# Strassen's scheme for the feed-forward up products: seven block products for two output tiles in place of eight

## What is computed

```python
def sq_relu_mlp(h, w_up, w_down):                 # first model, D_FF = 4096
    return jnp.square(jax.nn.relu(h @ w_up)) @ w_down
...
D_FF_2 = 2816                                     # second model
FFN_CONV = 3
```

## Time and profile before

| | |
|---|---|
| median of 3 runs | 2861.84 us (2861.54 to 2865.23) |
| the profiled execution, span | 2860.9 us |
| TensorE busy | 2799.9 us, 98% |
| weight loads (PEld) busy | 2463.7 us, 86% |
| POOL, DVE, ACT busy | 1376.9, 1479.0, 1000.0 us |
| granted TensorE clock | 0.993 of full speed over the span |

### The profile page before, as it was taken

One profiled execution on the slowest core, in us unless ns is written; L12 is line 12 of the kernel. 1 busy time (PEld: TensorE's weight loads), 2 busy tenths in 40 slices (PEclk: granted clock), 3 DMA queues, 4 the chain that ended last, 5 costly groups with the idle time before them and its releaser, 6 DMA issues.

```text
span 2860.9 us, 43560 instructions
## 1 busy us (share of the span) xinstructions
PE 2799.9 (98%) x17428; PEld 2463.7 (86%) x17428; DVE 1479.0 (52%) x2439; ACT 1000.0 (35%) x1489; POOL 1376.9 (48%) x1748
## 2 busy tenths in 40 slices
PE   9989999999999999999899999999999999999999
PEld 7768888877788888998799999999989799999887
DVE  8955322267532227897644544233798745444241
ACT  4453222255422224443353322223443345322221
POOL 6426554555654556542225555456542225555554
PEclk9999999999999999999999999999999999999999
DMA  5103322222232224223324222222322243332322
GB/s 187 60 25 103 102 96 89 97 97 79 96 96 92 96 99 126 98 74 98 85 83 142 88 89 92 94 85 93 113 81 78 65 118 116 98 102 89 102 90 74
DMA packets 122630, 270.79 MB, mean 95 GB/s; under 512 B 22864, under 2 KB 57040, under 8 KB 122192
## 3 DMA queue, kind: packets, MB, share of 16 engines
q1 hardware_dynamic: 73104, 245.98, 26.0%
q10 hardware_dynamic: 49344, 22.19, 2.8%
HBM read 249.52 MB, written 18.61 MB: 94 GB/s over the span
## 4 chain that ended last, share of the span: by engine, by line
PE 42%; issue 29%; POOL 24%; DVE 4%; POOLq 0%; ACT 0%; DMA 0%; ACTq 0%; DVEq 0%
PE acc L666 33%; POOL w_lo L638 24%; PE acc L1078 2%; PE acc L1059 2%; PE aux L1059 2%; PE aux L1092 1%; DVE index_score L2706 1%; DVE best L2699 1%; PE acc L1286 0%; PE aux L969 0%; PE acc L1092 0%; PE acc L920 0%; PE aux L1278 0%; PE aux L951 0%; PE acc L1148 0%
## 5 line engine op out<-in xcount | busy, mean ns | idle before, releaser
L638 POOL TENSOR_TENSOR w_lo<-w_raw,w_hi 128x256 fp32r<-128x256 f32 x1744 | 1376.7, 821 | 1467.8 <-ACT w_hi L1320 1467.0
L666 PE MATMUL acc<-n_hi,w_hi 128*128 128x264 f32 (+1 forms) x2824 | 756.9, 323 | 2.3 <-DVE index_k L2398 1.3
L666 PE MATMUL acc<-n_lo,w_hi 128*128 128x264 f32 (+1 forms) x2824 | 748.0, 320 | 0.0
L666 PE MATMUL acc<-n_hi,w_lo 128*128 128x264 f32 (+1 forms) x2824 | 746.0, 319 | 0.0
L1320 ACT ACTIVATE w_hi<-w_raw 128x1024 fp32r<-128x1024 f32 (+1 forms) x436 | 454.1, 1043 | 615.2 <-PE acc L666 561.5
L666 PEld LDWEIGHTS acc<-n_hi,w_hi 128*128 128x128 f32 x2824 | 470.4, 188 | 59.8 <-issue 15.0
L666 PEld LDWEIGHTS acc<-n_lo,w_hi 128*128 128x128 f32 x2824 | 467.3, 188 | 40.9 <-issue 2.6
L666 PEld LDWEIGHTS acc<-n_hi,w_lo 128*128 128x128 f32 x2824 | 467.2, 188 | 38.3
L2214 DVE TENSOR_TENSOR x<-x,acc 128x512 f32<-128x512 f32 (+1 forms) x144 | 99.7, 692 | 562.6 <-PE acc L666 519.3
L666 PE MATMUL acc<-hidden_lo,w_hi 128*128 128x512 f32 (+1 forms) x1040 | 343.3, 358 | 0.0
L666 PE MATMUL acc<-hidden_hi,w_lo 128*128 128x512 f32 (+1 forms) x1040 | 342.7, 357 | 0.0
(11 more groups left out here) (484 smaller groups left out, 3750.0 us busy)
## 6 DMA issues: line engine op xcount, KB each, us to landing
w_raw<-in_stream SPq DMA_DIRECT2D x420, 512.0 KB, 3.5
unit_blocks<-unit_scratch ACTq DMA_DIRECT2D x26, 256.0 KB, 4.0
w_raw<-in_stream SPq DMA_DIRECT2D x16, 384.0 KB, 3.0
unit_scratch<-unit_staged ACTq DMA_DIRECT2D x20, 256.0 KB, 2.8
saved_x<-x SPq DMA_DIRECT2D x2, 2112.0 KB, 10.5
x<-saved_x SPq DMA_DIRECT2D x16, 264.0 KB, 2.7
saved_gates<-root ACTq DMA_DIRECT2D x12, 264.0 KB, 2.1
unit_scratch<-unit_staged ACTq DMA_DIRECT2D x1, 2560.0 KB, 13.4
```

Source lines behind the costliest of these rows:

```text
L638: i = pool.tensor_tensor(wl[:, slot, s], raw[:, slot, s], wh[:, slot, s].bitcast(F32), ALU.subtract)
L666: last = pe.matmul(o, w[:, p % W_SLOTS, P * b:P * b + P], r, start=(b == 0 and i == 0), stop=(b == n - 1 and i == 2))
```

## The change

Two output tiles of an up product (in the second model a gate tile and its partner) are made together as a 2x2 block product: the weights of two pieces are four half pieces of four blocks each, a11 and a12 (first piece), a21 and a22 (second), and the rows are cut in two halves of 256 (264). In place of eight half products, seven are made (the form of Strassen's scheme with shared sums): with a11, a12 and a22, and with four sums of half pieces, s1 = a21 + a22, s2 = s1 - a11, s4 = a12 - s2, s3 = a21 - a11. DVE makes the weight sums (`weight_sum_of`) from the raw fp32 pieces, 128x512 each; ACT and POOL then split all seven as they split whole pieces before. The sums of the normed activations that the scheme needs are made once at each stage's start: 20 DVE instructions of 128x256 (264) (`token_sums`), four ACT copies and four DVE subtractions of 128x1024 (1056) (`token_sum_low`).

Three of the products serve two results. ACT copies them out of PSUM when they are done (`keep_product`), TensorE goes on adding to the same bank, and DVE makes results as bank plus kept copy (`pair_product`).

The ring now is in half pieces, eight of them (`Order`), and every "op" is a half piece of 12 matmuls' weight blocks. One pair is a11 s1 a12 s2 s4 s3, then the two halves of a down piece, then a22, and in the first model two more down halves. The hidden chunks have four tiles now, and a down piece holds half the rows for two output tiles, so that each down op is 12 matmuls of 512 columns (24 of 264 in `layer0`). The first four tiles of `mlp0` and `mlp1` and the first three of the second model's (six pieces) are made whole, as before. That leaves 14 pairs in each of `mlp0`, `mlp1` and 19 in each of `layer0`, `layer1`. In `layer1` both up halves are made for all 528 rows. POOL's loop is written out. The other stages keep their work; their waits are counted in ops.

A cut of the diff, with the loops of the second model's feed-forward (the first model's are alike, with relu and square):

```diff
--- before.py
+++ after.py
@@ -111,18 +111,29 @@
...
-def mlp_order():
...
-FFN_THIRDS = [(0, 8), (8, 16), (16, FT2)]
-FFN_ORDER = [("up", 0), ("up", 1), ("down", 0), ("up", 2), ("down", 1), ("down", 2)]
+MLP_CHUNKS = [(n, n + 4) for n in range(0, FF // P, 4)]
+FFN_CHUNKS = [(0, 3), (3, 6)] + [(n, n + 4) for n in range(6, FT2, 4)]
...
+def feed_steps(stage):
+
+    chunks, gated = chunks_of(stage), stage.startswith("layer")
+    order = [("whole", 0, n) for n in range((2 if gated else 1) * chunks[0][1])]
+    for e in range(1, len(chunks)):
+        n = (chunks[e][1] - chunks[e][0]) // (1 if gated else 2)
+        for i in range(n):
+            order.append(("pair", e, i))
+            order += [("down", e - 1, k) for k in range(4 * i // n, 4 * (i + 1) // n)]
+    return order + [("down", len(chunks) - 1, k) for k in range(4)]
...
+FACTORS = ("a11", "s1", "a12", "s2", "s4", "s3", "a22")
+SUMS = ("s1", "s2", "s4", "s3")
+LATER = 2
...
+        def add(kind, piece, part, halves=1):
+            nonlocal place
+            place += place % halves
+            self.turned.append(max(in_ring[(place + n) % (2 * W_SLOTS)] for n in range(halves)))
+            self.ops.append((kind, piece, part))
+            self.place.append(place % (2 * W_SLOTS))
+            for n in range(halves):
+                in_ring[(place + n) % (2 * W_SLOTS)] = len(self.ops)
...
+        for stage, end in zip(STAGES, ends):
+            feed = stage.startswith(("mlp", "layer"))
+            steps = feed_steps(stage) if feed else []
...
+                    add("whole", p, 0, 2)
+                    p += 1
+                elif what == "pair":
+                    self.op_of[p] = len(self.ops)
+                    for f in FACTORS[:6]:
+                        add(f, p, pair)
+                    kept = (p, pair)
+                    pairs.append(p)
+                    pair += 1
+                    p += 2
+                else:
+                    self.op_of[p] = len(self.ops)
+                    for part in range(2):
+                        add("down", p, part)
+                    p += 1
+                    if kept:
+                        add(FACTORS[6], *kept)
+                        kept = None
...
+        found = [n + 1 for n, (kind, piece, _) in enumerate(self.ops) if piece == p or (piece == p - 1 and kind == "a22")]
+        paired = [n + 1 for n, (kind, piece, _) in enumerate(self.ops) if piece == p and kind == "s3"]
+        return paired[0] if paired else max(found)
...
+    def weights_of(o):
+
+        kind, p, part = order.ops[o]
...
+        if kind in ("a11", "a12"):
+            return raw[:, p % RAW_SLOTS, half * (kind == "a12"):half * (kind == "a12") + half]
+        if kind == "s3":
+            return raw[:, (p + 1) % RAW_SLOTS, 0:half]
+        if kind == "a22":
+            return raw[:, (p + 1) % RAW_SLOTS, half:2 * half]
+        return weight_sum[:, SUMS.index(kind), :]
...
         for p in range(RAW_SLOTS, pieces):
-            sp.wait_ge(w_lo, p - RAW_SLOTS + 1)
+            sp.wait_ge(w_lo, order.freed(p - RAW_SLOTS))
...
+        for o, (kind, p, part) in enumerate(order.ops):
+            slot, at = order.half(o)
+            n = width_of(o)
+            source = weights_of(o)
+            pool.wait_ge(w_hi, o + 1)
+            for a in range(0, n, 2 * P):
+                z = min(a + 2 * P, n)
+                i = pool.tensor_tensor(wl[:, slot, at + a:at + z], source[:, a:z],
+                                       wh[:, slot, at + a:at + z].bitcast(F32), ALU.subtract)
+            i.then_inc(w_lo, 1)
...
+        def pairs_and_downs(stage, cols):
...
+            def banded(o, bank, hi, lo, opens):
+
+                slot, at_ = order.half(o)
+                for b in range(KT // 2):
+                    for i, (w, v) in enumerate(((wh, hi), (wh, lo), (wl, hi))):
+                        mm = pe.matmul(aux[:, bank, 0:width], w[:, slot, at_ + P * b:at_ + P * b + P], v[:, b, :],
+                                       start=(opens and b == 0 and i == 0), stop=(b == KT // 2 - 1 and i == 2),
+                                       skip_group_check=True)
+                mm.then_inc(w_used, 1)
...
+            for o in feed["ops"]:
+                kind, p, u = order.ops[o]
...
+                if kind == "a11":
+                    if u >= 2:
+                        pe.wait_ge(pair_out, out + 4 * (u - 1))
+                    banded(o, X_BANK[u % 2], nh[:, low, parts[0]], nl[:, low, parts[0]], True)
...
+                    banded(o, Y_BANK, nh[:, high, parts[0]], nl[:, high, parts[0]], True)
+                elif kind == "s2":
+                    if u == 0:
+                        pe.wait_ge(t_ready, sums + 2)
+                    pe.wait_ge(product_kept, kept + 3 * u + 1)
+                    banded(o, X_BANK[u % 2], th[:, 1, :, 0:width], tl[:, 1, :, 0:width], False)
+                elif kind == "s4":
+                    pe.wait_ge(product_kept, kept + 3 * u + 2)
+                    banded(o, Z_BANK, nh[:, high, parts[1]], nl[:, high, parts[1]], False)
+                elif kind == "s3":
...
+                elif kind == "a22":
+                    if u == 0:
+                        pe.wait_ge(t_ready, sums + 4)
+                    pe.wait_ge(pair_out, out + 4 * u + 3)
+                    banded(o, X_BANK[u % 2], th[:, 3, :, 0:width], tl[:, 3, :, 0:width], False)
...
+        def split_one():
+
+            o = at["split"]
+            kind, p, u = order.ops[o]
...
+                act.wait_ge(w_sum, c.next(w_sum))
...
+                act.wait_ge(landed[p % RAW_SLOTS], 16 * (p // RAW_SLOTS + 1))
+            if order.turned[o]:
+                act.wait_ge(w_used, order.turned[o])
+            n = width_of(o)
+            act.activation(wh[:, slot, at_:at_ + n], weights_of(o), ACT.Copy).then_inc(w_hi, 1)
+            at["split"] = o + 1
+
...
+        def split_before(o):
...
+            while at["split"] < len(order.ops):
                 q = at["split"]
...
-                at["split"] = q + 1
+                if order.turned[q] + (LATER if order.ops[q][0] in SUMS else 0) > o:
+                    return
+                split_one()
...
+        def token_sums_high(stage):
...
+            parts = halves_of(stage)
+            width = parts[0].stop - parts[0].start
+            for n in range(4):
+                act.wait_ge(t_sum, c.next(t_sum))
+                act.activation(th[:, n, :, 0:width], tf[:, n, :, 0:width], ACT.Copy).then_inc(n_hi, c.made(n_hi))
+
+        def keep_product(o, u, width):
+
+            kind = order.ops[o][0]
+            n = ("a11", "s1", "s2").index(kind)
+            act.wait_ge(w_used, o + 1)
+            if u:
+                act.wait_ge(pair_out, c.at(pair_out) + 4 * (u - 1) + (1, 3, 2)[n])
+            bank = Z_BANK if kind == "s1" else X_BANK[u % 2]
+            act.activation(kept_product[:, n, 0:width], aux[:, bank, 0:width], ACT.Copy)\
+                .then_inc(product_kept, c.made(product_kept))
...
+            for o in feed["ops"][:-KT]:
+                kind, p, u = order.ops[o]
+                split_before(o)
+                if kind in ("a11", "s1", "s2"):
+                    keep_product(o, u, HALF)
+                if kind == "s1" and u:
+                    hidden_high(whole + u - 1)
+                if kind == "s3":
+                    gate_silu(whole + u)
+            hidden_high(whole + feed["pairs"] - 1)
...
+            difference = [step(dve.tensor_tensor(t1[k], x[:, k, second], x[:, k, first], ALU.subtract)) for k in low]
...
+                made.append(ended(k, dve.tensor_scalar(t1[k], t1[k], gains(k), None, ALU.mult)))
...
+                made2.append(ended(k, dve.scalar_tensor_tensor(t2[k], x[:, high[k], second], gains(high[k]), t1[k],
+                                                               ALU.mult, ALU.subtract)))
...
+        def token_sum_low(stage, n):
+
+            width = halves_of(stage)[0].stop - halves_of(stage)[0].start
+            dve.wait_ge(n_hi, c.next(n_hi))
+            dve.tensor_tensor(tl[:, n, :, 0:width], tf[:, n, :, 0:width], th[:, n, :, 0:width].bitcast(F32), ALU.subtract)\
+                .then_inc(t_ready, c.made(t_ready))
...
+        def weight_sum_of(stage, u, name):
...
+                    dve.wait_ge(landed[q % RAW_SLOTS], 16 * (q // RAW_SLOTS + 1))
+            if name != "s3" and at["split"][n]:
+                dve.wait_ge(w_lo, at["split"][n])
+            at["split"][n] = order.index[name, p, u] + 1
...
+            s1, s2, s4 = (weight_sum[:, k, :] for k in range(3))
+            if name == "s1":
+                i = dve.tensor_tensor(s1, a21, a22, ALU.add)
+            elif name == "s2":
+                i = dve.tensor_tensor(s2, s1, a11, ALU.subtract)
+            elif name == "s4":
+                i = dve.tensor_tensor(s4, a12, s2, ALU.subtract)
+            else:
+                i = dve.tensor_tensor(a21, a21, a11, ALU.subtract)
+            i.then_inc(w_sum, c.made(w_sum))
```

(67 more changed lines are left out.)

705 lines of the change are left out of this document (469 added, 236 removed).

## The result

The changed kernel takes 2896.06 us (median of 4 runs, 2894.46 to 2899.78) against 2861.7 before (4 runs, 2861.54 to 2865.23): a ratio of 1.0125, 95% interval 1.0111 to 1.0140, or 34 us slower. Run again on another chip it took 2896.31 against 2860.88, 1.0127 [1.0112, 1.0143]. The forecast was 2906.

What follows compares the result with a forecast made beforehand. The prediction took TensorE to set the pace before the change, its share 100% in the feed-forwards. Forecast: 2861.8 - 24.4 + 15.6 + 26.6 + 20 + 6 + 0.9 = 2906.5, so 2906 us; range 2812 to 2948.

Steps and rivals of the forecast that it cites:

- first-model pairs: mlp0 and mlp1: each pair goes from 22.27 us to 21.4, TensorE needing 21.10; 28 pairs, -24.4 us.
- second-model pairs: layer0 and layer1: each pair takes 18.4 us, from 17.58 and 17.00; +15.6 and +26.6 us.
- four starts: Start of each feed-forward stage: DVE's queue of token sums and weight sums delays s3; 5 us each, +20.
- ends of stages: Last down products: DVE needs 0.85 us more than it gets, seven times in mlp1, +6; elsewhere 0 to +2.
- whole pieces: layer1's three pieces made whole, now at 264 columns: 72 slightly dearer matmuls, +0.9 us.
- narrow-matmul rival: 256-column matmuls can't go below 0.1221 us, so first-model pairs take 0.29 us more: 2915 us, chance 0.04.
- the port's 18.1: Second-model pair: POOL's 12.6 us and DVE's 5.5 on SBUF add up if they always take turns.
- The chain: Second-model pair: dependent DVE steps, then ACT's splits before the kept product's copy, then TensorE's s2 and s4: 18.8 us.
- The signs: Expected profile: first-model pairs 21.1 to 21.6 us, second-model 18 or more, POOL over 90% busy there, DVE's sums 1.2.
- TensorE bound: POOL and DVE mostly miss each other; second-model pairs take 16.1 and 15.9 us: 2788 us, chance 0.16.
- Full chain: All DVE's port instructions collide and waits add up; second-model pairs take 19.3 us: 2940 us, chance 0.20.
- Half way: Second-model pairs take some 17.2 us, with 15 us for the starts: 2856 us, chance 0.20.

Runs made afterwards that it cites:

- experiment 1: Changed kernel with ACT copying out the kept product before splitting the next half pieces, in the second model's pairs: 2887.2 us.
- experiment 2: Changed kernel with POOL making only half the low parts of the weights in the second model's pairs (result wrong, measures a cost): 2836.73 us.
- experiment 3: Changed kernel with the edits of experiment 1 and experiment 2 together (result wrong, measures a cost): 2829.75 us.
- experiment 8: Version 6 with DVE waiting at the start of mlp0 and mlp1 for POOL's low part of s1 before its next long instruction: 2859.82 us, 1.0000.
- experiments 4: Changed kernel with ACT allowed to split a weight sum one op earlier, all through: 2892.0 us.
- version 6: Changed kernel with the scheme in mlp0 and mlp1 only, layer0 and layer1 as before, and ACT's sum splits one op earlier: 2850.45 us, 0.9967.
- 7: Version 6 with DVE's weight sums moved earlier at the stage's start and ACT keeping products first in the first model too: 2852.78 us, 0.9972.
- experiment 9: Changed kernel with four fills with zeros in place of each stage's 20 token sums (result wrong, measures a cost): 2879.26 us.

## Why the prediction was right, and where its terms were off

The direction was right, and so was the mechanism of the largest term, the port that bounds the second model's pairs. That the total came within 10 us is luck: the pairs were 11 and 20 us better than forecast, and the starts 23 us worse.

| term | predicted | measured |
|---|---|---|
| first-model pairs, 28 | -24.4 | -35.6 |
| second-model pairs, 38 | +42.2 | +22 |
| four starts | +20 | +43 |
| ends of stages | +6 | +7.7 |
| whole pieces | +0.9 | not separable |
| unchanged stages | 0 | -3.7 |

*First-model pairs.* Measured 21.0 us, which is TensorE's 84 + 48 matmuls: 28 x (21.0 - 22.27) = -35.6. TensorE's 21.10 was right to 0.1 us, and 256 columns took 0.118 us. The 0.3 us for imperfect interleaving was not needed, with POOL at 92%. The narrow-matmul rival fell. The 98 ns for 256 columns, my estimate between the figures of the Trainium skill (TensorE: Matmul & The Clock Gate, "Back-to-back issue gap"), is contradicted by the measured 118 ns, and its 131 ns at 512 columns by the 232.

*Second-model pairs.* The port bounds them, as predicted, but at 17.3 us and not 18.4. This is the term that was mis-sized, in two steps. First, the shared time: with POOL full (experiment 1) a pair takes 17.1 us and not the port's 18.1, which is 12.6 of POOL's own and so 4.5 of DVE's 5.5; not all of DVE's instructions collided (L2701 kept 679 ns). The chain adds 0.2 us to that, where I had put 0.3 on the 18.1. (Its own list sums to 18.7 and not 18.8, and the 1.19 us read from the earlier trace rows is 0.1 less than the 0.70 and 0.59 of which it was said to be made; neither moves the forecast.) Second, I took all 19 pairs of a layer to have cost 17.58 or 17.00 us before; seven of them have down pieces of three blocks, which cost TensorE 16.12 and 15.61 (12 down matmuls of 264 columns fewer, or 6 of 512). The pair hardly shrinks with them (17.4 to 17.6), though the port isn't full there: POOL is busy 88% of the time (92.87 us from 1661 to 1766 us), and experiment 1 takes 108.7 us for six of the seven to 104.9, experiment 2 to 94.8. What holds these seven is port and chain together, in shares that no run separates. So twelve pairs changed by -0.28 and +0.35 us each, -3 and +4 us, and nearly all of the loss, +9 and +12, is in the seven (which hold eight down pieces), where TensorE would have needed only the 14.6 of experiment 3.

*Starts.* Predicted 5 us each. Measured 10 to 12: in `mlp0` 10.0 of holes and 1.7 of clock, in `mlp1` 8.7 and 3.0, in `layer0` and `layer1` about 10 each (a hole of 3.5 while DVE makes token sums and takes no accumulator, the clock in `layer0`, and a first pair 5.1 and 6.5 us longer than the next). I had counted DVE's queue in sum and allowed for slower instructions; its 20 token sums took 8.3 us in `mlp0` and 11.4 in `layer0`, where I had 6.8. Not in the count were ACT's queue (s1 waited 4.2 us behind the third tile's square), POOL shut out by the unbroken run of DVE, which costs not a turn but the length of the run, and the clock behind the hole. What came was my upper bound of 10 a start, or more.

*Ends.* Less a matmul's own spacing, matmuls begin 3.5 us later in sum at `mlp1`'s end (predicted 6); before the last down products TensorE waits 2.08 us in `layer0` and 2.49 in `layer1` for the hidden low part, where I had 0 to 2 for all stages but `mlp1`.

The measured terms sum to +33.4 us, and the spans differ by 33.3.

*The signs.* Of what would show it, POOL over 90% busy (97%), its instructions of 0.9 to 1.2 us, TensorE idle before s2 for the kept product and first-model pairs near 21.1 came. Second-model pairs of 18 us or more did not, and only two of the four sums took 1.2 us.

*The rivals.* TensorE bound: not so in the second model; experiment 3 shows what it would have given there (2829.75). Full chain: its parts are there, at 0.2 us a pair. Half way is the rival whose pair (17.2 us) was all but measured, and yet not its time (2856): it too took the old cost of all pairs at 17.58 and 17.00, and 15 us for the starts. By its pairs alone it was nearer the truth than the forecast.

## What to carry to other kernels

When a change trades matmuls for elementwise work, add up for each pair of engines that share the SBUF port what both need in one period, and compare it with what TensorE will need after the change, in the period where TensorE needs least and not in the average one: here 17.4 us a pair with POOL at 88%, against the 14.6 that TensorE needed, in seven pairs of nineteen. Use such a trade only where the other engines have the room (here the first model: -0.3%), and look at each stage's start by itself, where two thirds of what all the pairs save (17.8 us in `mlp0`) are given back, 11.7 us. A run of DVE instructions with two SBUF inputs each, one close behind the other, held POOL off here for up to 5.3 us, so a short instruction of POOL's on the critical path wants a pause or a PSUM-reading instruction of DVE's beside it; but a pause made with a wait delays all that is queued behind it.

## What the hardware showed that was not expected

**DVE's unbroken run keeps POOL out.** In the pairs the two engines take turns (L2697 1220 ns and POOL 933 to 1060). The Trainium skill says that a DVE instruction with two SBUF inputs and a GpSimd one that reads SBUF contend, by an exclusive lock (SBUF — State Buffer, "Who interferes with whom"), and the trace agrees in that neither ran beside the other. At the stage's start there are no turns: POOL's two instructions took 4.60, 6.34 and 6.86 us while DVE kept its free lengths, and 1.41 us with DVE held (experiment 8). One instruction of POOL's alone stood for 5.31 us behind DVE's with SBUF inputs, although it had begun before all but the first of them, and in the changed kernel and experiments 4, 6 and 7 the longest of these instructions (2.80 and 5.31 us) ended together with DVE's next PSUM-reading one, to within 0.02 us. No run here shows what decides between turns and shutting out.

**After holes of 5 to 12 us TensorE came back at the low clock.** Behind each such hole of the changed kernel and of versions 6 and 8 it was granted 0.50 to 0.57 for 4 us or more, and 16 to 20 matmuls of 256 columns started in 4 us. In version 6, after its hole of 7.05 us:

```profile
268.00:272.00 4.00, 4.00 (x20) 4.00 (x21) 3.27 (x5) 1.92 (x2) 4.00 (x4) 0.50 0.00 0
```

After a hole of 4.98 us (experiment 9, `mlp1`) it was 0.50 too, while the 3.5 us hole of `layer1` left 1.00 and the one of `layer0` 0.64. A short hole is no safe one: in version 6 one of 2.17 us follows at 272.8 us, and the clock, by then back at full, fell again just behind it:

```profile
276.00:280.00 4.00, 4.00 (x23) 4.00 (x22) 3.83 (x6) 1.18 (x4) 4.00 (x7) 0.57 0.42 135
```
